# GEMM matmuls that read their moving operand from the last column to the first and write their results in that order

## The chip, the cores and the metric

The kernel runs on one core of a Trainium2 chip. The metric is the device time of one execution in microseconds (us). All weights are in the chip's HBM when it starts, and the result is written back to HBM.

## The reference, cut to what matters

The program is a stack of transformer-like blocks on a sequence of 512 rows with a model width of 1024, in float32. Two layers of a first block run one after the other, then one layer of a second block. Each is a chain of dense products with small stages between them:

```python
for layer in range(2):
    x = x + 0.5 * swiglu_ffn(rms_norm(x, g1), w_gu, w_down)      # 1024 -> 2*2816 -> 1024
    h = rms_norm(x, g2)
    x = x + (even_mixer if layer == 0 else odd_mixer)(h, w_in, ..., w_out)
    x = x + memory_cross_attention(rms_norm(x, g3), rms_norm(mem, g4), w_q, w_kv, ..., w_o)
    x = x + 0.5 * swiglu_ffn(rms_norm(x, g5), w_gu2, w_down2)
# second block: one wide projection (recurrent branch, sparse attention branch, two gates),
# their output projections, w_o, then one more swiglu_ffn
```

A GEMM here is one of these dense products of activations with a weight matrix from HBM. The products inside attention, the transposes and the small sums are not GEMMs in this sense.

## The kernel before, in words

The GEMMs of PE (TensorE) take their operands as fp32r, a float32 with a rounded mantissa. The kernel splits every operand in two: a high part, rounded to fp32r, and a low part, the difference to the original. A product is then the sum of three matmuls: high by high, low by high and high by low.

Weights stream in chunks of 256 rows by up to 512 columns. SP issues the transfers into four buffers `raw` (`sp_weights`). ACT copies each chunk to `wh` (high), DVE subtracts to get `wl` (low), each with four buffers (`act_split`, `dve_split`). Activations lie transposed in `hTh` and `hTl` (or `F..h` and `F..l` for the hidden layer of a feed-forward stage, `s_Y..`, `s_Z..` and `c0m..`, `c1m..` for others): 128 rows of the model width by 512 sequence positions, for each of 8 or 22 such tiles.

All GEMMs go through one function, `pe_products`. For each group of output columns it walks over the chunks, over the two 128-row halves k of a chunk, over up to four output banks j, and over the three products q. Two forms exist. In form "A" a 128 by 128 block of weights is stationary and 512 sequence positions of the activation move; in form "B" 128 positions of the activation are stationary and up to 512 weight columns move. Either way one matmul fills up to 512 float32 columns of one PSUM bank, that is the whole 2 KiB of it, and all matmuls of one bank accumulate over k and q. Two sets of four banks alternate from group to group, so that ACT and DVE empty one (`evict`) while PE fills the other.

The order of work on each engine is written out by hand. An engine waits on semaphores: PE for `w_lo` (the chunk's low part), `hi_done` and `lo_done` (the activation's parts) and `drained` (the bank is emptied). The last matmul into a bank raises `summed`, on which the eviction waits, and the last one that reads a chunk raises `w_used`, on which the next copies into its buffers wait.

Line 94 is the helper through which all matmuls pass, line 97 the one for transposes. In the profile's names the moving operand stands first behind the arrow: `ps<-hTh,wh` is form "A" (hTh moves, wh is stationary), `ps<-wh,hTh` is form "B".

One other access of the kernel runs backwards. In stick-breaking attention (`breaks`, line 1246) DVE makes a cumulative product from the last key to the first, in place, through the view `T_.keep(g, u, i)[:, ::-1]`. The trace has it as TENSOR_TENSOR_SCAN `evQ<-evQ,evZ`. Its second input is a single zero, repeated. The forward scan of the recurrent branch is `s_ri<-s_ra,s_th`.

Of the kernel before, what the change touches and what calls it, by code (L numbers as in the profile page):

```python
# [265 lines left out]
def program(nc, T, out):  # L266
# [10 lines left out]
    bank = [ctx.enter_context(nc.psum_tensor(f"ps{i}", [P, 512], F32)) for i in range(8)]  # L277
# [78 lines left out]
    def blocks_of(name, g):  # L356

        _, K, groups = spec[name]
        got = [[kp] for kp in range(K // 2)]
        if g == len(groups) - 1 and name not in BESIDE:  # L360
            got[-2:] = [[K // 2 - 2, K // 2 - 1]]
        return got
# [92 lines left out]
    def pe_gemm(pe, name, acts, side=lambda g, kp: None):  # L455
        for _ in pe_products(pe, name, acts, side):
            pass

    def pe_products(pe, name, acts, side=lambda g, kp: None):

        _, K, groups = spec[name]
        n = first[name]
        for g, segs in enumerate(groups):
            jobs, o = [], 0
            for _, _, width, a, form in segs:
                A = acts[a]
                if form == "A":
                    jobs += [(A, "A", slice(o + j * P, o + (j + 1) * P), slice(0, A.n)) for j in range(width // P)]
                else:
                    jobs += [(A, "B", slice(o, o + width), slice(t * P, (t + 1) * P)) for t in range(A.n // P)]  # L470
                o += width
            for block in blocks_of(name, g):
                for u in range(len(block)):
                    pe.wait_ge(w_lo, n + u if n else "half")
                ks = [(2 * kp + kk, n + kp - block[0], kk) for kp in block for kk in range(2)]
                order = [(k, j, range(3)) for k in ks for j in range(len(jobs))] if len(block) == 1 else \
                        [(k, j, range(3)) for j in range(len(jobs)) for k in ks]
                if not g and len(block) == 1:

                    order = [(k, j, qs) for k in ks for qs in ([range(3)] if k[0] == K - 1 else [range(2), range(2, 3)])  # L480
                             for j in range(len(jobs))]
                for (k, m, kk), j, qs in order:
                    A, form, wc, tc = jobs[j]
                    b = home[name, g] + j
                    if m == 0 and kk:
                        pe.wait_ge(w_lo, 0)
                    if 0 in qs:
                        pe.wait_ge(hi_done, (A.key, k, 0))
                    if k == 0 and 0 in qs:
                        if b in pe.held:  # L490
                            pe.wait_ge(drained, pe.held[b])
                        pe.held[b] = (name, g, j)
                    Wh, Wl = wh[m % NW][:, kk, wc], wl[m % NW][:, kk, wc]
                    Ah, Al = A.hi[:, k, tc], A.lo[:, k, tc]
                    M = (wc.stop - wc.start) if form == "B" else A.n
                    full, used = k == K - 1, kk == 1 and j == len(jobs) - 1
                    parts = ((Wh, Ah), (Wl, Ah), (Wh, Al)) if form == "A" else ((Ah, Wh), (Ah, Wl), (Al, Wh))
                    for q in qs:
                        if q == 2:
                            pe.wait_ge(lo_done, (A.key, k))  # L500
                        p0, p1 = parts[q]
                        ins = pe.matmul(bank[b][:, 0:M], p0, p1, start=k == 0 and q == 0, stop=k == K - 1 and q == 2)
                        if q == 2 and full:
                            ins.then_inc(summed, (name, g, j))
                            if used:
                                ins.also(w_used, m)
                        elif q == 2 and used:
                            ins.then_inc(w_used, m)
                        yield
                for kp in block:  # L510
                    side(g, kp)
                n += len(block)
            side(g, None)
# [187 lines left out]
    def pe_f1u0(pe):  # L701
        pe_warm(pe, home["f1u0", 0], 14)
        pe_turn_x(pe, range(2))
        side = rates_side(pe_rates, pe, "f1u0")
        for i, _ in enumerate(pe_products(pe, "f1u0", {"h": hT("f1u0")}, side), 1):
            if i == 12:
                pe_turn_x(pe, range(2, 4))
            elif i == 36:
                pe_turn_x(pe, range(4, KD))
                leave(pe, "f1u0")  # L710
# [968 lines left out]
    def pe_in0(pe):  # L1679
        def side(g, kp):  # L1680
            if g == 2 and kp == 0:
                pe_turn(pe, "in0", 0, e_ta, 4, NT, 1)
            if g == 2 and kp == 2:
                pe_turn(pe, "in0", 1, e_kd, 2, NT)
            pe_rates(pe, "in0", g, kp)
        return pe_products(pe, "in0", {"h": hT("in0")}, side)
# [1289 lines left out]
```

## Time and profile before

| what | value |
|---|---|
| median of 2 timed runs | 3130.33 us (3130.27 to 3130.39) |
| profiled execution | span of 3127.9 us; its time outside the span isn't given |
| instructions | 37166 |
| PE matmul | 3112.8 us busy, 14504 matmuls |
| PE weight load | 2517.6 us |
| DVE, ACT, POOL | 1581.5, 1219.4 and 318.7 us |
| DMA | 290.95 MB, 93 GB/s in the mean |

The profile is that of one execution. Its page gives busy time for each engine, the same in 40 slices, the DMA queues, the chain of work that ended last, and the costliest groups of instructions. A matmul's duration runs from its start to the modelled end of its last column, so that consecutive matmuls overlap; the distance between their starts shows how fast they flow. Further views list single instructions in order of time, waits, or the busy time in chosen stretches.

### The profile page before, as it was taken

The numbers are of one execution on the slowest core, as the hardware profiler recorded it, in microseconds if no ns is written. First come the engines' busy times: TensorE is split into PE (matmuls) and PEld (weight loads), VectorE is DVE, ScalarE is ACT, GpSimd is POOL, SyncE is SP. The second block draws the span as 40 slices with busy tenths as digits, with TensorE's granted clock in tenths as the row PEclk, the third lists the DMA queues.
The fourth block names the chain that finished last, engine by engine and source line by source line (L and its number), as shares of the span: only waits on it lengthen the run. The fifth ranks groups of instructions, "written<-read, shape, count | busy, mean of one in ns | idle before, by whom it ended". The sixth has DMA issues, their size and how long they took to land. (4 is left out here: it accounts for less than half of the span.)

```text
span 3127.9 us, 37166 instructions
## 1 busy us (share of the span) xinstructions
PE 3112.8 (100%) x14504; PEld 2517.6 (80%) x14504; DVE 1581.5 (51%) x2479; ACT 1219.4 (39%) x1994; POOL 318.7 (10%) x454
## 2 busy tenths in 40 slices
PE   9999999999999999999999999999999999999999
PEld 8888886878888888888866878888887786788887
DVE  5443358754444344433566754443346876564433
ACT  4332247543232233223455543322335727443222
POOL 1000114211000000001210200000142200020000
PEclk9999999999999999999999999999999999999999
DMA  5333331412332333333222413332232231223332
GB/s 159 94 95 101 96 94 35 148 61 88 101 101 95 95 95 94 101 98 97 89 95 82 148 48 101 95 101 95 86 101 81 77 108 33 84 86 95 99 97 74
DMA packets 214368, 290.95 MB, mean 93 GB/s; under 512 B 13072, under 2 KB 138384, under 8 KB 214064
## 3 DMA queue, kind: packets, MB, share of 16 engines
q1 hardware_dynamic: 211120, 279.26, 28.6%
q0 software_dynamic: 2496, 8.98, 0.9%
q8 instruction: 114, 1.87, 0.2%
q14 instruction: 62, 0.51, 0.1%
q10 hardware_dynamic: 576, 0.33, 0.0%
HBM read 286.42 MB, written 2.10 MB: 92 GB/s over the span
## 5 line engine op out<-in xcount | busy, mean ns | idle before, releaser
L103 DVE TENSOR_TENSOR wl<-raw,wh 128x1024 fp32r<-128x1024 f32 (+2 forms) x531 | 654.1, 1239 | 1068.2 <-ACT wh L100 1064.3
L100 ACT ACTIVATE wh<-raw 128x1024 fp32r<-128x1024 f32 (+2 forms) x531 | 552.1, 1048 | 1142.9 <-PE ps L94 1103.8
L94 PE MATMUL ps<-hTh,wh 128*128 128x512 f32 x2400 | 942.1, 393 | 0.7 <-ACT hTh L100 0.7
L94 PE MATMUL ps<-hTh,wl 128*128 128x512 f32 x2400 | 938.0, 391 | 0.0
L94 PE MATMUL ps<-hTl,wh 128*128 128x512 f32 x2400 | 895.6, 391 | 0.2 <-DVE hTl L109 0.2
L94 PEld LDWEIGHTS ps<-hTh,wh 128*128 128x128 f32 x2400 | 450.8, 188 | 101.8 <-issue 9.9
L94 PEld LDWEIGHTS ps<-hTh,wl 128*128 128x128 f32 x2400 | 450.8, 188 | 97.3 <-issue 7.1
L94 PEld LDWEIGHTS ps<-hTl,wh 128*128 128x128 f32 x2400 | 449.4, 188 | 96.9 <-issue 4.7
L103 POOL TENSOR_TENSOR xn<-xn 128x512 f32<-128x512 f32 x69 | 99.2, 1438 | 1769.1 <-ACT xn L100 1531.7
L94 PE MATMUL ps<-wh,hTh 128*128 128x512 f32 (+2 forms) x576 | 216.8, 377 | 0.0
L94 PE MATMUL ps<-wl,hTh 128*128 128x512 f32 (+2 forms) x576 | 215.1, 374 | 0.0
L94 PE MATMUL ps<-wh,hTl 128*128 128x512 f32 (+2 forms) x576 | 195.1, 374 | 0.0
L94 PEld LDWEIGHTS ps<-wh,hTh 128*128 128x128 f32 x576 | 108.3, 188 | 20.1 <-issue 2.2
L94 PEld LDWEIGHTS ps<-wl,hTh 128*128 128x128 f32 x576 | 108.4, 188 | 19.1 <-issue 1.4
L94 PEld LDWEIGHTS ps<-wh,hTl 128*128 128x128 f32 x576 | 107.2, 188 | 20.3 <-issue 1.8
L109 DVE SCALAR_TENSOR_TENSOR hTl<-xT,prm,hTh 128x512 fp32r<-128x512 f32 x72 | 75.5, 1056 | 15.2 <-ACT hTh L100 14.2
L100 ACT ACTIVATE hTh<-xT,prm 128x512 fp32r<-128x512 f32 x72 | 51.2, 716 | 69.0 <-DVE xT L109 39.8
L94 PE MATMUL ps<-wh,f3Fh 128*128 128x512 f32 x176 | 68.8, 391 | 0.0
L94 PE MATMUL ps<-wl,f3Fh 128*128 128x512 f32 x176 | 68.5, 389 | 0.0
L94 PE MATMUL ps<-f10Fh,wl 128*128 128x512 f32 x176 | 68.5, 389 | 0.0
L94 PE MATMUL ps<-f20Fh,wl 128*128 128x512 f32 x176 | 68.5, 389 | 0.0
L94 PE MATMUL ps<-f21Fh,wl 128*128 128x512 f32 x176 | 68.5, 389 | 0.0
(418 smaller groups left out, 4005.2 us busy)
## 6 DMA issues: line engine op xcount, KB each, us to landing
raw<-in_ffn_w_gu SPq DMA_DIRECT2D x350, 256.0 KB, 3.1
raw<-in_ffn_w_down SPq DMA_DIRECT2D x88, 512.0 KB, 3.5
raw<-in_xa_w_kv SPq DMA_DIRECT2D x32, 512.0 KB, 3.9
raw<-in_w_in SPq DMA_DIRECT2D x28, 512.0 KB, 3.7
raw<-in_od_w_in SPq DMA_DIRECT2D x24, 512.0 KB, 3.6
raw<-in_w_ffn_gate SPq DMA_DIRECT2D x44, 256.0 KB, 2.8
raw<-in_w_ffn_up SPq DMA_DIRECT2D x44, 256.0 KB, 3.1
raw<-in_w_ffn_down SPq DMA_DIRECT2D x22, 512.0 KB, 3.8
```

The lines of the kernel that those rows point to most:

```text
L94: return self.made(lambda e: e.matmul(*a, **k))
L100: return self.made(lambda e: e.activation(*a, **k))
L103: return self.made(lambda e: e.tensor_tensor(*a, **k))
L109: return self.made(lambda e: e.scalar_tensor_tensor(*a, **k))
```

## The change

In the matmul of `pe_products` the output and the moving operand are given as views with a step of -1. The stationary operand and the flags stay as they are. Column i of the moving operand still ends in column i of the bank; only the order in which the columns are visited is turned round, the last one first. The view `[:, 0:M]` is 512, 292 or 256 columns wide.

```diff
--- before.py
+++ after.py
@@ -499,7 +499,7 @@
                         if q == 2:
                             pe.wait_ge(lo_done, (A.key, k))
                         p0, p1 = parts[q]
-                        ins = pe.matmul(bank[b][:, 0:M], p0, p1, start=k == 0 and q == 0, stop=k == K - 1 and q == 2)
+                        ins = pe.matmul(bank[b][:, 0:M][:, ::-1], p0, p1[:, ::-1], start=k == 0 and q == 0, stop=k == K - 1 and q == 2)
                         if q == 2 and full:
                             ins.then_inc(summed, (name, g, j))
                             if used:
```

## Rows read from the trace of the kernel before

**Rows 1.** The page: busy time by engine, and the span in 40 slices.
```profile
PE 3112.8 (100%) x14504; PEld 2517.6 (80%) x14504; DVE 1581.5 (51%) x2479; ACT 1219.4 (39%) x1994; POOL 318.7 (10%) x454
...
PE   9999999999999999999999999999999999999999
...
PEclk9999999999999999999999999999999999999999
```

**Rows 2.** Waits of PE on other engines: total us, times, longest us.
```profile
PE ps L94 <- ACT evQ L100: 4.4, 4, 2.2
PE ps L94 <- POOL rc L103: 1.2, 1, 1.2
```

**Rows 3.** The chain that ended last, its end: start us, us, what.
```profile
3119.79 0.02 issue
...
3124.82 0.66 DVEq L2896
```

**Rows 4.** Windows, matmuls that read wh: us, PE busy (count), clock, DMA share, GB/s.
```profile
0.00:3128.00 3128.00, 2542.02 (x8224) 1.00 0.30 93
```

**Rows 5.** Windows, the same for the matmuls that read wl.
```profile
0.00:3128.00 3128.00, 1595.12 (x4112) 1.00 0.30 93
```

**Rows 6.** Groups by form: count | busy us, mean ns | idle before.
```profile
L94 PE MATMUL ps<-hTh,wh 128*128 128x512 f32 x2400 | 942.1, 393 | 0.7 <-ACT hTh L100 0.7
...
L94 PE MATMUL ps<-wh,hTh 128*128 128x292 f32 x64 | 18.4, 297 | 0.0
...
L94 PE MATMUL ps<-wh,hTh 128*128 128x256 f32 x32 | 9.1, 285 | 0.0
...
L115 DVE TENSOR_TENSOR_SCAN s_ri<-s_ra,s_th 128x512 f32<-128x512 f32 x8 | 12.6, 1579 | 0.3
...
L115 DVE TENSOR_TENSOR_SCAN evQ<-evQ,evZ 128x512 f32<-128x512 f32 x8 | 10.1, 1263 | 0.0
```

**Rows 7.** PE in order of time, last up projection: first and last of 26 matmuls.
```profile
2784.15 0.39 PE L94 MATMUL ps<-hTh,wh 128*128 128x512 f32 x1
...
2789.82 0.39 PE L94 MATMUL ps<-hTh,wl 128*128 128x512 f32 x1
```

**Rows 8.** Tile f11Fh, third down projection: ns min/median/max, first and last start.
```profile
L94 PEld LDWEIGHTS ps<-f11Fh,wl x176: 187/188/188, 1353.6 to 1472.6; 128*128 128x128 f32 x176
L94 PE MATMUL ps<-f11Fh,wl x176: 389/389/390, 1353.8 to 1472.8; 128*128 128x512 f32 x176
```

**Rows 9.** PE in order of time, 256 columns: first and last of 18 matmuls.
```profile
399.90 0.28 PE L94 MATMUL ps<-wh,hTl 128*128 128x256 f32 x1
...
401.94 0.28 PE L94 MATMUL ps<-wl,hTh 128*128 128x256 f32 x1
```

**Rows 10.** PE in order of time, 292 columns: first and last of eight matmuls.
```profile
2256.77 0.29 PE L94 MATMUL ps<-wh,hTh 128*128 128x292 f32 x1
...
2257.70 0.29 PE L94 MATMUL ps<-wl,hTh 128*128 128x292 f32 x1
```

**Rows 11.** Tile s_ri: the forward scan, ns min/median/max.
```profile
L115 DVE TENSOR_TENSOR_SCAN s_ri<-s_ra,s_th x8: 1224/1224/2172, 2421.6 to 2497.2; 128x512 f32<-128x512 f32 x8
```

**Rows 12.** PE in order of time, plain fp32 matmuls of cross attention.
```profile
692.22 3.62 PE L94 MATMUL ps<-c0kT,c0qT 128*128 128x256 f32 x16
695.67 1.04 PE L97 MATMUL ps<-misc,cx0P 128*128 128x128 f32 x8
696.55 3.60 PE L94 MATMUL ps<-cx0PT,c0v 128*128 128x512 f32 x8
699.98 1.04 PE L97 MATMUL ps<-misc,cx0P 128*128 128x128 f32 x8
```

**Rows 13.** PE in order of time, the first GEMM matmuls behind small fp32 ones.
```profile
2780.43 1.13 PE L94 MATMUL ps<-misc,rc 128*128 128x128 f32 x8 [1.21 <-POOL rc L103]
2781.32 0.48 PE L94 MATMUL ps<-hTh,wh 128*128 128x512 f32 x1
2781.63 0.39 PE L94 MATMUL ps<-hTh,wl 128*128 128x512 f32 x1
```

## Prediction

> **What bounds the kernel now.** I read the page's busy shares first: PE is busy for 3112.8 us of a span of 3127.9 us, while DVE is at 51% and ACT at 39%, and the sliced rows show PE at 9 in every slice and its granted clock at 9 or more in all 40 [rows 1]. A busy PE can still be a slow or a waiting one, so the wait list comes next: the largest item in which PE waited for another engine is 4.4 us in four times [rows 2]. Nothing outside PE sets the time, but for the first microsecond and for the last 8 us, which the chain of what ended last gives to ACT, DVE, POOL and the final transfer [rows 3]. So the time is a sum over PE's instructions, and what counts is how far apart they start, not the "mean ns" of a group, which overlaps the next one.
>
> How much of that sum do the changed instructions hold? Every GEMM matmul reads either wh or wl. The windows of these two tiles hold 8224 and 4112 matmuls [rows 4, 5]: 12336 of PE's 14504. All of them come from line 502, so the change touches every one. By width, 192 have 292 columns (64 in each of three groups), 96 have 256 (32 in each of three), and the other 12336 - 192 - 96 = 12048 have 512 [rows 6].
>
> Start to start, a 512-column one takes 0.2268 us: 26 of them start between 2784.15 and 2789.82, so 5.67/25 [rows 7]. The same comes from a whole stage: in the third down projection the matmuls on wl run from 1353.8 to 1472.8, which is 525 steps (three matmuls for each of 175) in 119.0 us, 0.2267 [rows 8]. The 256-column ones step by 0.120 us (399.90 to 401.94 is 17 steps in 2.04) and those of 292 by 0.133 (2256.77 to 2257.70, 7 steps in 0.93) [rows 9, 10]. From 256 to 512 columns the step grows by 0.1068 us, or 0.417 ns a column: one column for each cycle of 2.4 GHz, which is the upper of the two levels and agrees with the granted clock of 1.00 in the windows [rows 4, 5]. What is left over is 0.2268 - 512 x 0.000417 = 0.0133 us, the fixed part of each matmul. Summed: 12048 x 0.2268 + 192 x 0.133 + 96 x 0.120 = 2732.5 + 25.5 + 11.5 = 2769.5 us, 89% of the span. The rest, some 358 us, is attention, transposes, sums and the two ends, and isn't touched.
>
> **The change part by part.** It adds no instruction and removes none; no wait, buffer, bank, transfer or order between instructions is moved. All three products of a chunk go through the same line, so within one accumulation column 511 is always first and column 0 last: each element gets its addends in the same order from the same weights. The stationary operand p0 isn't reversed, so the weight loads (0.188 us each, beside the matmuls) stay as they are [rows 8]. Eviction waits for a semaphore that is raised when a whole matmul is done, so ACT and DVE don't see in which order the columns came. Copies into hTh, hTl, wh and wl are awaited as whole instructions as well, so that no matmul can start sooner or later on account of the end at which it begins. The queues of SP, ACT, DVE and POOL are untouched. These parts cost nothing, and since no cover is used up, there is none to lose.
>
> What remains is one price: d, by which the step of a matmul changes when its moving operand is read at a step of -1 and its output is written at -1. As PE is the bound throughout, each nanosecond of d is 12336 x 0.001 = 12.3 us, 0.39% of the time, with nothing in front of it that could hide it. No matmul of this trace has a negative step, so I bound d from the nearest rows.
> - Nearest in kind: the only accesses at -1 in the kernel are the in-place scans of DVE on line 1246. At 512 columns they take 1263 ns in the mean [rows 6]; the forward scans s_ri have a median of 1224 ns and a mean of 1579, though they read two full streams where these read one [rows 6, 11]. Reading and writing backwards costs DVE next to nothing there. It is a weak witness: a scan spends 2.4 ns on an element, so a halved memory rate could hide under it, and DVE isn't PE.
> - Upper end: matmuls of plain fp32 have the same columns and weights' shape, and move half as many columns in a time: in the cross attention 8 of 512 columns take 3.43 us (696.55 to 699.98), 0.429 each, and 16 of 256 take 3.45 us, 0.216 each [rows 12]. That is 0.84 ns a column at the same granted clock. If columns in reverse went one at a time through a stage that now takes two, this is what the step would be: d = 0.429 - 0.227 = 0.202 us at 512.
> - Between: a restart for each matmul. The first GEMM matmul behind the small fp32 ones at 2781.32 holds the next one off until 2781.63, 0.31 us against 0.227: 0.083 more [rows 13]. A second fixed part of 0.0133 is the small version of this.
> - Below nothing: all that d could give back is the fixed 0.0133 us, 164 us in total. No row hints that the direction has anything to do with it.
>
> I take d = 0. The rate seen is what a stream gets in which neighbouring elements follow each other, and in the reversed one they still do: the neighbours 511 and 510 lie side by side as 0 and 1 did, and an even count of columns pairs up from either end. The row nearest to the question, DVE's, has no penalty. The sum is then 3127.9 + 0 for the span. The page gives the profiled execution its span alone; the median of the two timed runs is 3130.33, 2.4 us more, so the forecast is 3130 us.
>
> A rule bears on this. PE moves 0.417 ns a column into PSUM while both patterns step by +1 [rows 7, 9]. The Trainium skill, "PSUM — Partial Sum Buffer", section "Specifications (TRN2)", says that cachelines there are 8 bytes and that "any non-contiguous AP slows matmuls significantly"; two fp32 columns are 8 bytes. Read strictly, -1 isn't contiguous, and the rule speaks against this change; read by its reason, two columns in reverse still fill one line, and nothing is lost. No matmul in this trace writes PSUM in steps, so the trace can't choose.
>
> **Rivals.**
> 1. Columns singly (the slower side). Place: PE's read of the moving operand or its write to PSUM, where pairs are formed only at a step of +1. It decides from the first matmul on; no second condition is needed. Price from the plain fp32 rows [rows 12]: 12048 x 0.202 = 2434 us, 192 x (292 x 0.00084 - 0.133) = 22 us, 96 x (0.216 - 0.120) = 9 us, in total 2465 us: 5595 us, +79%. For it: the step at the full clock is so close to one column a cycle that any lost pairing must show. Against: a general pattern with its own start and step for each operand is part of the instruction, and DVE follows one at no extra price. This would be the result of the strict reading of the PSUM page.
> 2. A fixed or per-line penalty for each matmul: from 0.0133 us (164 us in all, 3295 us) to the restart of 0.083 us (12336 x 0.083 = 1024 us, 4154 us), with DVE and ACT more idle than before. For it: an odd first address such as column 511 is new to PE here. Against: 25 steps in a row show no spread [rows 7], so nothing is on the verge of waiting. The Trainium skill, "SBUF — State Buffer", section "Specifications (TRN2)", gives 16-byte lines there and a penalty at each cross to a new line; both directions cross as many.
> 3. Faster: the fixed part shrinks or goes. At most 164 us, 2966 us. Nothing speaks for it.
> 4. The reversal doesn't reach the chip, because both patterns flipped together mean the same product and something normalises them. The time is that of my forecast; only the patterns in the trace would tell.
>
> **How the numbers follow.** d = 0: 0.66. Normalised away: 0.02. Columns singly: 0.21. Fixed or per-line penalty: 0.09, nearly all of it over 2% (2% is 62.6 us, d = 5.1 ns), and 2% is about what a measurement of this kernel can tell from no change. Faster: 0.02. So faster by over 2% 0.02, within 2% 0.68, slower 0.30. The forecast's own range would be 3115 to 3145 us, since the added terms are all nought and only run-to-run spread and small knock-ons are left. But it holds under 7 in 10, and the small penalty brings it to 0.77; to leave out no more than 2 in 10 the range has to take in the doubled column time, which is the unknown cost's upper end. It goes from 3115 to 5620 us.
>
> **What would show it.** If I am right: 512-column GEMM matmuls still start 0.227 us apart, PE stays near 3113 us busy at clock 1.00, and waits on others keep their size. Singly: a step of about 0.43 us at 512 and 0.22 at 256, DVE's share falling from 51% to about 28%, PE still full. A penalty per matmul: the step at 256 and at 512 grows by the same amount; per line, in the ratio of the widths. Faster: a step under 0.2268. What would make the forecast wrong is just one thing, a price of direction in PE's paths that no row of this trace can show; a change in another engine's time would mean that I misread who sees the order of columns.

## The result, and the profile after

The changed kernel takes 3205.53 us (median of 2 runs, 3204.8 to 3206.26) against 3130.33 us: a ratio of 1.0239, 95% interval 1.0217 to 1.0261. It is slower by 75 us, where I had forecast no change. In the comparisons below the kernel before was run again beside each experiment and took 3130.4 to 3130.7 us beside the timed ones.

The page after, busy time by engine, to be held against [rows 1]:

```profile
PE 3188.4 (100%) x14504; PEld 2520.1 (79%) x14504; DVE 1581.8 (49%) x2479; ACT 1218.3 (38%) x1994; POOL 316.7 (10%) x454
...
PEclk9999999999999999999999999999999999999999
```

PE's busy time grew by 75.6 us and the span by 75.1 (3127.9 to 3203.0), with the same 14504 matmuls at the same granted clock. No other engine took longer by as much as 1 us; PE's own weight loads (PEld) sum to 2.5 us more. The waits of PE are those of before within 0.2 us as well, to be held against [rows 2] (total us, times, longest):

```profile
PE ps L94 <- ACT evQ L100: 4.4, 4, 2.2
PE ps L94 <- POOL ones L139: 1.1, 1, 1.1
PE ps L94 <- POOL rc L103: 1.0, 1, 1.0
```

So the matmuls flow more slowly. Tile f11Fh of the changed kernel, the third down projection, answers to [rows 8] (ns min/median/max, first and last start):

```profile
L94 PEld LDWEIGHTS ps<-f11Fh,wl x176: 188/188/188, 1387.4 to 1509.9; 128*128 128x128 f32 x176
L94 PE MATMUL ps<-f11Fh,wl x176: 397/397/398, 1387.6 to 1510.1; 128*128 128x512 f32 x176
```

The same 525 steps take 122.5 us where they took 119.0: 0.2333 us each against 0.2267. At 2.4 GHz these are 560 and 544 cycles for 512 columns. Less one cycle for each column that leaves 48 and 32 cycles, which I call cycles "over the width" from here on. The weight load keeps its 188 ns. PE in order of time shows that not all widths pay; first and last of 26 matmuls of 512 columns, of 18 with 256 and of 8 with 292, to be held against [rows 7, 9, 10]:

```profile
2855.13 0.40 PE L94 MATMUL ps<-hTh,wh 128*128 128x512 f32 x1
...
2860.96 0.40 PE L94 MATMUL ps<-hTh,wl 128*128 128x512 f32 x1
...
406.04 0.28 PE L94 MATMUL ps<-wh,hTl 128*128 128x256 f32 x1
...
408.05 0.28 PE L94 MATMUL ps<-wl,hTh 128*128 128x256 f32 x1
...
2309.13 0.30 PE L94 MATMUL ps<-wh,hTh 128*128 128x292 f32 x1
...
2310.06 0.30 PE L94 MATMUL ps<-wl,hTh 128*128 128x292 f32 x1
```

At 512 columns 5.83/25 = 0.2332 us against 0.2268; at 256, 2.01/17 = 0.118 against 0.120; at 292, 0.93/7 = 0.133 as before. The whole price is thus 0.0067 us for each of 12048 wide matmuls: 80 us, where 75 were measured.

Where the other 5 us stayed can be read from single starts, since both traces hold the 14504 matmuls in the same order and can be matched one by one. The step after a wide matmul grew by 6.6 ns in the 11001 cases in which ten or more wide ones stand before it in a row, by 3.2 ns in the 871 nearer to a matmul of another kind or width, and not at all in the 175 right before one. A stream thus pays in full only when it has settled.

### The profile page after: what moved, and what is told of

Read it like the earlier page. It is cut to its first block and busy times, and to the rows that moved or that the text cites. A ratio compares the mean times of both kernels' runs of the same rounds, so it can differ in the third digit from the quotient of the medians.

```text
span 3203.0 us, 37166 instructions
## 1 busy us (share of the span) xinstructions
PE 3188.4 (100%) x14504; PEld 2520.1 (79%) x14504; DVE 1581.8 (49%) x2479; ACT 1218.3 (38%) x1994; POOL 316.7 (10%) x454
## 5 line engine op out<-in xcount | busy, mean ns | idle before, releaser
L94 PE MATMUL ps<-hTh,wh 128*128 128x512 f32 x2400 | 961.2, 401 | 0.7 <-ACT hTh L100 0.7
L94 PE MATMUL ps<-hTh,wl 128*128 128x512 f32 x2400 | 957.1, 399 | 0.0
L94 PE MATMUL ps<-hTl,wh 128*128 128x512 f32 x2400 | 914.3, 399 | 0.0
L94 PE MATMUL ps<-f21Fh,wh 128*128 128x512 f32 x176 | 69.9, 397 | 0.0
L94 PE MATMUL ps<-f10Fh,wh 128*128 128x512 f32 x176 | 69.9, 397 | 0.0
L94 PE MATMUL ps<-f20Fh,wh 128*128 128x512 f32 x176 | 69.9, 397 | 0.0
```

The lines of the kernel that those rows point to most:

```text
L94: return self.made(lambda e: e.matmul(*a, **k))
```

## The experiments

Two questions were open: is it the read or the write that costs, and why only at 512 columns? I had these theories. A: the price lies in the read of the moving operand; A1, because that read meets the read of the next weights; A2, because a reversed read starts more dearly. B: the write to PSUM. C: it takes both, or the two directions must differ. D: collisions with other engines.

### Read and write apart: e1_read_only, e2_write_only

```diff
+ins = pe.matmul(bank[b][:, 0:M], p0, p1[:, ::-1], ...)          # e1
+ins = pe.matmul(bank[b][:, 0:M][:, ::-1], p0, p1, ...)          # e2
```

> The kernel before, with only the moving operand read from its last column to its first; the results are written forwards, so the columns of every GEMM come out in reverse order and the output is not the reference's. Theory A (the price lies in the read of the moving operand): about 3205 us, a step of 0.2333 us between 512-column matmuls. Theory B (the price lies in the write to PSUM): about 3130 us, a step of 0.2267 us. Theory C (it takes both, or a mismatch of the two directions costs more): anything else, above 3205 us above all.

> The kernel before, with only the results written from the last column of the bank to the first; the moving operand is read forwards, so again the columns come out in reverse order. Theory A (read): about 3130 us, step 0.2267 us. Theory B (write): about 3205 us, step 0.2333 us. Were both to hold a part, the two runs would add up to the 75 us.

Measured: e1 3205.57 us, ratio 1.0241 (1.0211 to 1.0271); e2 3130.72 us, ratio 1.0001 (0.9990 to 1.0013). In the third down projection, tile f11Fh, e1 has the steps of the changed kernel and e2 those of before:

```profile
L94 PE MATMUL ps<-f11Fh,wl x176: 397/397/398, 1387.6 to 1510.1; 128*128 128x512 f32 x176
```
```profile
L94 PE MATMUL ps<-f11Fh,wl x176: 389/389/390, 1353.9 to 1472.9; 128*128 128x512 f32 x176
```

They take 122.5 and 119.0 us for 525 steps. All of the cost is in the read, and writing PSUM backwards costs nothing that can be measured here. B is out, and C with it, as e1 takes what both together take.

### PE alone: m1_pe_alone

A kernel of its own: fixed tiles, groups of N = 48 fp32r matmuls, nothing beside them. Each group alternates between two moving tiles so that the trace keeps the groups apart.

```diff
+for i, (M, way, d, o) in enumerate(cf):
+    m = mv[i % 2][:, 128:128 + M]
+    for n in range(N):
+        k = 128 * (n % 4) + d
+        dst = bank[n % 4][:, o:o + M]
+        a, b = m, dst
+        if way[0] == "r":
+            a = a[:, ::-1]
+        if way[1] == "r":
+            b = b[:, ::-1]
+        ins = e.matmul(b, w[:, k:k + P], a, start=True, stop=True)
```

> Not the reference's computation: PE alone runs groups of 48 fp32r matmuls from fixed tiles, with no DMA, ACT or DVE work beside them, in widths 512, 384, 292, 256 and 128, with read and write forwards or backwards in all four ways, and at 512 and 256 with the weights' address moved against the moving operand's by 16 to 384 bytes. Theory A1 (the read of the moving operand collides with the reads of the weight load beside it, which is a matter of the two address streams): the step at 512 is 0.2267 forwards and 0.2333 in reverse at no shift, and changes with the shift in at least one direction, by some 7 ns or more. Theory A2 (a fixed start-up of a reversed read): 0.0067 more in reverse at every width and every shift. Theory B (the write): the step follows the write's direction alone. Theory D (collisions with ACT, DVE or DMA): no difference between the directions here, where PE is alone.

PE in order of time; each row is a group, and the distance between two starts, divided by 48, is a step. The first four rows: read and write reversed; read alone; write alone; the group after, 384 columns forwards, whose start closes the third. Then, forwards and with the weights moved by 64 bytes, 512 columns and the group after, and 256 columns and the group after; last, 512 columns forwards without a shift, and its successor:

```profile
19.28 11.37 PE L59 MATMUL ps<-mvb,wgt 128*128 128x512 f32 x48
30.48 11.36 PE L59 MATMUL ps<-mva,wgt 128*128 128x512 f32 x48
41.69 11.06 PE L59 MATMUL ps<-mvb,wgt 128*128 128x512 f32 x48
52.58 8.51 PE L59 MATMUL ps<-mva,wgt 128*128 128x384 f32 x48
...
178.33 11.36 PE L59 MATMUL ps<-mva,wgt 128*128 128x512 f32 x48
189.53 11.40 PE L59 MATMUL ps<-mvb,wgt 128*128 128x512 f32 x48
...
345.93 5.61 PE L59 MATMUL ps<-mva,wgt 128*128 128x256 f32 x48
351.38 5.93 PE L59 MATMUL ps<-mvb,wgt 128*128 128x256 f32 x48
...
448.37 11.04 PE L59 MATMUL ps<-mva,wgt 128*128 128x512 f32 x48
459.25 11.37 PE L59 MATMUL ps<-mvb,wgt 128*128 128x512 f32 x48
```

Both reversed (30.48 - 19.28)/48 = 0.2333, read alone 0.2335, write alone 0.2269; forwards, 459.25 - 448.37, 0.2267. PE alone has the whole effect, so D is out. And the row at 178.33 is the surprise: forwards in everything, but with the weights 64 bytes further on, the step is (189.53 - 178.33)/48 = 0.2333 too. The direction is only one way of coming to this number. Worked out from all groups, cycles over the width:

```
weights ahead of moving by, bytes    0   16   32   64   96  128  192  256  384
512 columns, forwards               32   36   48   48   50   46   38   34   46
512 columns, reversed               48   48   48   48   48   48   48   48   48
256 columns, forwards               31   28   28   16   32   29   26   32   28
256 columns, reversed               28   26   26   27   27   32   32   28   32
width (no shift)         512  384  292  256
forwards                  32   34   28   31
reversed                  48   43   28   29
```

These are means of whole groups, and a group that follows one of another kind has a run-in of some ten matmuls. Single starts show the rest: at 512 columns forwards, 0, 16 and 256 bytes all settle at 0.2267 us, 32 cycles over, and so does a width of 384. Elsewhere the same case can come out 2 cycles apart (46 here, 48 in m2 at 128 and at 384 bytes).

The favourable place isn't the same for all widths. With the weights 64 bytes on, where 512 columns pay the full 48, 256 columns have their best step, (351.38 - 345.93)/48 = 0.1135 us or 16 over, and m3 repeats it. Even the 32 cycles at 256 columns were no constant.

A2 asked for 16 more at every width and is out; A1's "changes with the shift in at least one direction" came true forwards.

### The same in the real kernel: e3_shift_forward, e4_shift_reverse

```diff
-    raw = [...]
+    xn_at = nc.sbuf_base
+    xn = [sb(f"xn{i}", [P, D]) for i in range(2)]
+    raw = [...]
+    sb("shift", [P, 16])
     wh = [...]
```

The two lines of xn go from behind wl to here. e3 is this edit on the kernel before, e4 on the changed one. Against what the expectation says, the small tiles that are allocated behind the weights (misc, prm and others) move by 64 bytes too; they carry none of the time, since in e3 the steps from one matmul outside the GEMMs to the next sum to 289.5 us against 290.2 before.

> The kernel before, forwards in everything, with all weight tiles moved 64 bytes further against the activations (the scratch tiles xn are allocated ahead of them to make room; all other tiles stay). Theory A1: the 9696 wide matmuls whose stationary operand is a weight tile go from a step of 0.2267 to 0.2333 us, as in the single test at 64 bytes, which alone makes 3195 us; with those in which the weights move as well it is up to 3211 us. Theory A2 or any theory that hangs on the direction: 3130 us.

> The changed kernel (reversed) with the same move of the weight tiles by 64 bytes. Theory A1 with what the test of PE alone showed (0.2333 us in reverse at every shift): 3205 us, the same as the changed kernel. If the shift mattered in reverse too, the time would go off 3205 us by up to 75 us either way. A2: 3205 us as well; this run tells A1's two directions apart, not A1 from A2.

Measured: e3 3195.55 us, ratio 1.0207 (1.0177 to 1.0237), without one reversed access in its GEMMs; e4 3206.77 us, 1.0243 (1.0213 to 1.0273). The matmuls on wl of e3 in the third down projection (form A) and in the last one (form B; weights move), of tiles f11Fh and f3Fh:

```profile
L94 PE MATMUL ps<-f11Fh,wl x176: 393/393/398, 1385.0 to 1507.5; 128*128 128x512 f32 x176
```
```profile
L94 PE MATMUL ps<-wl,f3Fh x176: 388/388/398, 3062.6 to 3186.6; 128*128 128x512 f32 x176
```

Form A has 122.5 us for its 525 steps, the full price; form B's stage, in which four runs of transposes stand between the matmuls, takes 124.0 us, between the 122.6 of before (2999.3 to 3121.9) and the 126.0 reversed (3071.0 to 3197.0). That fits m1: where the weights are what moves, their shift puts the stationary operand 64 bytes behind, which is 192 ahead in a pattern that repeats after 256 (see m2), and 38 cycles in place of 32 are 1.3 us for 525 steps. The address of the weights alone can cost forwards what the reversal costs; in reverse it changes the time by 1.2 us.

### Streams, widths and orders: m2_pe_streams, m3_pe_orders, m4_widths_places

The same loop as in m1 with other cases.

> Not the reference's computation: PE alone again, 48 fp32r matmuls of 512 columns for each case, from fixed tiles. (a) Forwards, with the weights' address 0 to 496 bytes ahead of the moving operand's in steps of 16 bytes, and 4, 8 and 12 bytes. (b) Stationary operand of 128, 96, 64 and 32 columns, forwards and reversed. (c) The moving operand in blocks of 256 to 4 columns, the blocks in reverse order with the columns inside forwards, or the other way round. Theory A1 (the moving read collides with the read of the next weights, so what counts is how many weights are read beside it and how the two address streams meet): in (b) the part over 512 cycles, 32 forwards and 48 in reverse, falls with the number of stationary columns, to about 16 and 24 at 64; in (a) it swings between about 32 and 48 with a period. Theory A2 (a dearer start of a reversed read): in (b) the difference of 16 cycles stays whatever the stationary operand's width. In (c) A1 says that blocks of 4 columns (16 bytes) reversed inside cost as little as forwards, since lines follow each other as they did, and lines in reverse order cost what the full reversal costs; A2 would charge any negative step.

> Not the reference's computation: PE alone, 48 matmuls for each case. (a) fp32r, 512 columns, with the 16-byte groups of four columns visited in strides of 2 to 64 groups, and in blocks of 16 and 64 columns turned round: is there an order with a step under 0.2267 us? I expect 0.2267 to 0.2333 for all. (b) Both streams moved together by 16 to 128 bytes: if only the distance between the two addresses counts, 0.2267 for all four; if their absolute place does, it varies. (c) The moving operand alone moved by 16, 32 and 64 bytes: the mirror of moving the weights, so about 0.2267 to 0.2333. (d) The weights 96 KiB further away at the same place within 512 bytes: 0.2267 and 0.2333 if only the low address bits count. (e) bf16 operands forwards and reversed at five distances: if the meeting of weight load and moving read costs, bf16, which moves half the bytes, should cost less over 512 cycles and have a smaller difference between the directions. (f) Plain fp32, which takes 0.43 us for 512 columns: no difference, as its columns come at half the rate.

> Not the reference's computation: PE alone, 48 fp32r matmuls for each case. (a) Widths from 272 to 512 columns, forwards and reversed: the earlier cases gave 28 to 31 cycles over the width at 256 and 292 in both directions, 33 and 42 at 384, 32 and 48 at 512. If the reversed read loses something at a steady rate, its surplus over forwards climbs evenly with the width; if it loses a fixed number of slots at a certain point of the stream, it steps up once or twice and is flat between. (b) Both streams moved together by 16 to 256 bytes, both directions: forwards some places at 32 and some at 48 cycles over; reversed 48 at all if the reversed read can nowhere have the better meeting. (c) Reversed at eight more distances: 48 in all, or one with 32, which would make the change free of cost there.

In m2 a block is a run of neighbouring columns, and four of them are 16 bytes. From m2, PE in order of time: stationary operands of 96, 64 and 32 columns, in each pair forwards first, then reversed; then blocks of four columns, first the blocks in reverse order, then the columns inside them, then all forwards, then all reversed:

```profile
430.19 11.21 PE L56 MATMUL ps<-mva,wgt 128*96 128x512 f32 x48
441.24 11.36 PE L56 MATMUL ps<-mvb,wgt 128*96 128x512 f32 x48
452.44 11.20 PE L56 MATMUL ps<-mva,wgt 128*64 128x512 f32 x48
463.48 11.36 PE L56 MATMUL ps<-mvb,wgt 128*64 128x512 f32 x48
474.68 11.28 PE L56 MATMUL ps<-mva,wgt 128*32 128x512 f32 x48
485.80 11.36 PE L56 MATMUL ps<-mvb,wgt 128*32 128x512 f32 x48
...
586.28 11.37 PE L56 MATMUL ps<-mva,wgt 128*128 128x512 f32 x48
597.48 11.06 PE L56 MATMUL ps<-mvb,wgt 128*128 128x512 f32 x48
608.38 11.04 PE L56 MATMUL ps<-mva,wgt 128*128 128x512 f32 x48
619.26 11.37 PE L56 MATMUL ps<-mvb,wgt 128*128 128x512 f32 x48
```

Here A1 missed. Reversed, the group takes the same with 96, 64 and 32 weight columns: (474.68 - 463.48)/48 = 0.2333 at 64, 48 cycles over and not 24. Forwards, fewer columns make it worse, not better: 40 cycles at 96 and at 64, 44 at 32, against 32 at 128. So the 48 isn't a toll for each weight read beside the matmul. It looks more like the ordinary state, out of which 128 weight columns at a favourable place lift the forward read; this picture is a guess that no run tests. Over the shift, the forward scan in steps of 16 bytes repeats itself after 256 bytes: 32 to 33 at 0, 16, 240 and 256, 48 to 50 over most of the rest, 44 at 80, 38 to 40 at 176 and 192. Shifts of 4, 8 and 12 bytes gave 46, 42 and 40.

The last four rows are the other lesson. Blocks of four columns (16 bytes) with the columns inside reversed step by 0.2271, as forwards; the blocks in reverse order, forwards inside, by 0.2333. In larger blocks, each read forwards, the reverse order costs with blocks of 8 to 32 columns (46 to 49) and no longer with 64, 128 and 256 (33 to 34, which settle at 32). The other way round, blocks in forward order with the columns inside reversed, the cost isn't even: 48 with blocks of 8, 64, 128 and 256 columns, but 64 with 32 and 128 with 16 (m3), more than for the full reversal.

m3 looked for an order below 32 and found none: strides of 2 to 64 groups of four columns gave 31.5 to 156, the best being a stride of four groups, equal to plain forwards. Moving both streams together by 16 bytes gave 48, where it would be 32 if only their distance counted; by 32, 64 and 128 bytes 33 to 35, which settle at 32 to 33. m4 adds 43 to 48 at 48, 80 and 112 bytes and 34 to 35 at 160, 192 and 256. So the absolute place counts as well as the distance: multiples of 32 bytes are the good ones. Moving the activation alone isn't quite the mirror of moving the weights: 44, 48 and 37 at 16, 32 and 64 bytes, where the same distances had 33, 48 and 38. With the weights 96 KiB away it was 32 forwards. Reversed, the whole group comes out at 60, but only by the border to another type behind it: its starts at 359.81 and 365.64 us are 25 matmuls apart, 0.2332 us or 48 over, as near by. Groups of m3 (48 matmuls each; the trace holds 47 records of a bf16 group, and two for each matmul in plain fp32): bf16, reversed with the weights 16 bytes on, then forwards and reversed with 32 bytes, and in plain fp32, forwards and reversed:

```profile
399.77 10.52 PE L85 MATMUL ps<-mbx,mbw 128*128 128x512 bf16 x47
410.13 10.52 PE L85 MATMUL ps<-mby,mbw 128*128 128x512 bf16 x47
420.49 10.52 PE L85 MATMUL ps<-mbx,mbw 128*128 128x512 bf16 x47
...
472.29 41.36 PE L85 MATMUL ps<-mpy,mpw 128*128 128x512 f32 x96
513.49 41.36 PE L85 MATMUL ps<-mpx,mpw 128*128 128x512 f32 x96
```

bf16: 10.36/48 = 0.2158 us in both directions, 6 cycles over the width, and the same at the other distances (but for the first forward group, 0.211, at the border to another type). Plain fp32: 41.20/48 = 0.858 for a pair of passes either way. Neither minds the direction. A record of plain fp32 is thus one of two passes.

m4: up to 336 columns both directions lie within 6 cycles of each other at 27 to 33 over. From there the reversed read climbs unevenly: 38 at 352, 33 at 368, 38 at 400, 43 at 416 and 432, 48 at 448, 43 at 464 and 48 from 480. That is neither a steady rate nor one step. Forwards it climbs too, 38 to 41 from 432 to 496 columns, and then drops back to 32 at 512. In reverse, every further place of both streams (7) and every further distance (8) gave 48. The one reversed group off 48 is in m3, with the activation moved by 8 bytes: 53.

### The two orders in the real kernel: e5_in_line, e6_line_order

```diff
+dst, p1 = (v.rearrange("p (a b) -> p a b", b=4)[:, :, ::-1] for v in (bank[b][:, 0:M], p1))   # e5
+dst, p1 = (v.rearrange("p (a b) -> p a b", b=4)[:, ::-1, :] for v in (bank[b][:, 0:M], p1))   # e6
+ins = pe.matmul(dst, p0, p1, ...)   # both
```

> Every GEMM matmul reads its moving operand, and writes its output, with a step of -1 again, but only inside groups of four columns (16 bytes); the groups follow each other forwards. The output is the reference's. If what costs is the order in which 16-byte pieces are fetched, and not a negative step: 3130 us, step 0.2267 us (PE alone showed 0.2271). If any negative step costs, or the split into groups does: 3205 us or more.

> The opposite: inside each group of four columns forwards at a step of +1, and the groups from the last to the first. If the order of the 16-byte pieces costs: 3205 us, step 0.2333 us. If the negative step from element to element did it: 3130 us.

Measured: e5 3130.63 us, 1.0000 (0.9989 to 1.0011), with every GEMM read and write at a step of -1 from element to element inside its groups of four; e6 3205.81 us, 1.0241 (1.0211 to 1.0271), with none. What costs is the order in which the 16-byte pieces are read; the sign of the step inside them has no price.

### Half the dose: e7_form_a

```diff
+way = slice(None, None, -1) if form == "A" else slice(None)
+ins = pe.matmul(bank[b][:, 0:M][:, way], p0, p1[:, way], ...)
```

> Only the GEMM matmuls of form A are reversed (activation moves, weights stationary: 9696 of 512 columns); form B stays forwards. If each wide matmul pays its own 0.0067 us: 3130.5 + 9696 x 0.0067 = 3195 us, the other 10 us belonging to form B. A price that comes from another place, such as the queue or the whole stage, would not divide by count.

Measured: 3191.55 us, 1.0195 (1.0166 to 1.0225), 61 us of the 75. Against 9696 x 0.0067 = 65 us that is a little less, as the 75 are against 80: the steps near a matmul of another kind pay half or nothing, as the matched traces of before and after show. The 2300 steps of the wide form B matmuls to a next GEMM matmul, which stay forwards, grew by less than 0.1 us in all. The price divides by count.

## Why the prediction was wrong

**What bounds the kernel** held. PE was the bound, nothing covered the price, and the 75.6 us by which PE's busy time grew came out in the span as 75.1. So did "each nanosecond of d is 12.3 us": 75.1 us are 6.1 ns over 12336 matmuls.

**That everything but d costs nothing** held: same waits, same engines' times, same granted clock.

**The step that failed is "I take d = 0"**, and in it the two reasons given. Measured, d is 0.0067 us at 512 columns, nothing at 292 and 2 ns less than nothing at 256. "The neighbours 511 and 510 lie side by side as 0 and 1 did" is true and e5 shows that it is enough within 16 bytes; but the read also depends on how one 16-byte piece follows the other, and e6 shows that this alone is worth 75 us. And the row that I called nearest, DVE's backward scan, spoke of another engine at 2.4 ns an element; it couldn't show an effect of 0.013 ns a column. I had called it a weak witness and followed it.

**Rival 2**, the penalty for each matmul, was the right case with the wrong price and reason. I bounded it from 13 to 83 ns, by a second fixed part and by a restart; it is 6.7 ns at 512 and nothing at 256 and 292. So neither of its two signs came, the same growth at both widths or growth in their ratio. My case against it, that 25 equal steps show nothing on the verge of waiting, misread the rows: the 0.0133 us "fixed part" in them was already a loss of this sort, at a favourable place. bf16 has 6 cycles where these have 32. I took it for a constant of the engine because 256 and 512 columns agree in it; m4 shows that the widths between don't, 496 having 40, and m1 has 256 columns at 16.

**Rival 1**, single columns, is out on both sides. Its price was too low besides: the plain fp32 rows [rows 12] hold two records for each matmul, as m3 shows, so that 0.429 us is one pass and the matmul takes 0.858. e2 measures the write at -1 at no price. The Trainium skill, "PSUM — Partial Sum Buffer", section "Specifications (TRN2)", says that a non-contiguous pattern slows matmuls significantly; read strictly, so that -1 is one, the rule isn't borne out here. Writes that skip columns weren't run apart from such reads.

On the read side the Trainium skill, "SBUF — State Buffer", section "Specifications (TRN2)", speaks of 16-byte cachelines and a penalty for each cross to a new one. e5 and e6 agree with the unit: inside 16 bytes the order is free and beyond them it isn't, until the blocks reach 256 bytes. The price isn't one for each cross, of which both directions have 127; it depends on the order of the pieces and on where the weights lie. I had used the equal number of crossings as an argument against the rival.

**Rivals 3 and 4**: nothing got faster but the 96 matmuls of 256 columns, by 2 ns each, and the reversal reached the chip, since the time moved by 75 us.

**The chances** put 0.68 within 2%, on the ground that 2% is about what can be told from no change. The interval of the result is 0.2% to either side, so that also a d of 1 ns would have shown. That 3205.5 us lies between 3115 and 5620 is luck: the upper end is the price of rival 1, which is out.

**What is shown and what is open.** Shown: the cost is in the read of the fp32r moving operand, in the order of its 16-byte pieces; PE alone has it; forwards it depends on the address of the stationary operand too, which only the weight load reads; at 512 columns the kernel before sits at one of the places where the loss is 32 cycles and not 37 to 50; the reversed read found no such place in some 25 shifts of weights, moving operand or both. Open: why. A toll for each weight read was my theory and m2 refuted it, since the reversed loss is the same with 32 weight columns as with 128. Whether both reads going the other way round would restore the meeting wasn't tried: the order of the stationary operand was the same in all runs.

## What to carry to other kernels

When PE is the bound, read its step (distance of starts, in cycles, less the columns) and ask whether it is the least that this form has, before taking it for a constant: here 32 of 544 cycles were over the width, and 48 at most other placements. For fp32r at 512 columns, keep moving operands and weight tiles at the same place within 256 bytes, on multiples of 32, walk each 256-byte piece forwards, and recheck the step when a buffer is added in front of them: 64 bytes of padding cost this kernel 65 us. At other widths measure again, as 256 columns did best 64 bytes off. A reversed write to PSUM and a reversed order inside 16 bytes cost nothing here.

## What the runs showed of the hardware that I had not expected

- At the granted clock of 1.00 back-to-back fp32r matmuls of 512 columns with a weight load each, read forwards or fully reversed, settle at starts 544 to 562 cycles apart (565 at one 8-byte shift), bf16 ones at 518. The Trainium skill, "TensorE: Matmul & The Clock Gate", section "Back-to-back issue gap", gives N/2.4 + 2.5 ns for an isolated matmul, which is 215.8 ns at 512, and about 131 ns for a sustained stream. The back-to-back bf16 groups agree with the first (0.2158 us) and not with the second; the fp32r ones of before and after take 0.2267 and 0.2333.
- Some orders are far dearer: visiting groups of four columns at a stride of 16 groups (256 bytes) costs 0.278 us a matmul, 156 cycles over the width, in either direction.
- 128 columns of fp32r start 0.111 us apart, 266 to 268 cycles, twice their width.
